# Gate projection of a decoder layer as 2x2x2 blocks with Strassen's seven products

## The chip, the cores and the metric

One core of one Trainium2 chip. The metric is the time on the device, in microseconds, of one execution of the whole program. All data are fp32.

## The reference, cut to what matters

The program is one decoder layer for 512 prompt tokens and 8 sample tokens (520 columns in all, `TOK`). Only the part around the change:

```python
xn = rmsnorm(x, lw['norm1'])
proj = xn @ lw['w_in']            # 1024 features in; q, k, v, ssm and memory columns, then 3072 gate columns
...
gates = sigmoid(proj[..., GATE_COL:]).reshape(bsz, seq, 3, D_MODEL)
merged = gates[:, :, 0] * (att @ w_att_out) + gates[:, :, 1] * (ssm @ w_ssm_out) + gates[:, :, 2] * (mem @ w_mem_out)
h = x + merged @ lw['w_o']
...                               # then a router and 32 experts (w1, w3, w2: 201 MB of weights)
```

## The kernel before, in words

Every engine has one instruction list, written out by hand; semaphores order them, and each engine takes its list strictly in order. SBUF is one tile, `arena`, with places given in KB; PSUM is one tile, `bank`, of 8 banks. Tokens lie on the free axis (520 columns, two halves of `HALF` = 260), features on the partitions.

1. **Projection** (PE line 679): 26 column tiles of 128 by `x_tiles`, then the memory keys and values (line 771), and the S5 branch with its gated unit (lines 782 to 845), with side work on ACT, DVE and POOL.
2. **Gate stage with attention.** The 24 gate tiles (3072 columns) are worked off by `gate_tile` (lines 849 to 858): 8 feature blocks of the weights times two token halves, 16 products of 128x128 by 128x260, which accumulate in banks 0 and 1. ACT copies the tile out in `gate_out` (line 1406) to `gates`. 16 of them stand between the steps of the prompt's attention, two to each of 8 head pairs (lines 901 to 907: `gate_tile`, `turn_probs`, `gate_tile`, `scores` of the next pair, `values`); the other 8 stand between the steps of memory attention, one to each of 8 pairs (lines 921 to 941). The softmax of each pair runs beside a gate tile: on DVE lines 1756 to 1775 (two heads: add the distances, maximum, and after ACT's Exp of line 1413 the scaling of line 1775), in memory attention lines 1796 to 1807. SP loads each gate tile's weights (512 KB) into one of two `ring` buffers (line 439). POOL copies the caches of sample tokens 4 to 7 from DRAM to DRAM beside the first 16 gate tiles (`shift_caches`, line 537, whose waits count `tile`). ACT loads the caches for decode (`load_keys`, lines 398 and 399) after each of the first five memory pairs, and `w_ssm` (2 MB, line 1446) after the sixth.
3. **Decode attention.** ACT applies the sigmoid to all gates in one instruction (line 1450). PE goes through the cached keys of 8 sample tokens (lines 971 to 976), then the values (lines 1004 to 1014), with the S5 output products `ssm_out` (line 952) between them; DVE multiplies those by the gates (`ssm_merge`, line 1814), which frees the banks (`Sfree`). SP loads the later keys, values and output weights (lines 442 to 463).
4. **Output products and merge** (line 1032, DVE lines 1814, 1867, 1868), then `w_o` (line 1041), the norm and router, and the **experts** (lines 1165 to 1203), whose weights SP streams into ten buffers (`HOMES`); the first of them is loaded once the last `ssm_out` is done (line 465), the next once `merged` is complete (line 470).

A row of an fp32 matmul in the trace is half of one: each product of 128x128 by 128x260 has two rows, so that a gate tile has 32.

Of the kernel before, what the change touches and what calls it, by code (L numbers as in the profile page):

```python
# [32 lines left out]
P = 128  # L33
D = 1024
# [43 lines left out]
N_FIRST = N_PROJ + N_MEMT  # L78

# [47 lines left out]
def build(nc, t):  # L127

    with ExitStack() as ctx:
# [98 lines left out]
        kv_dec = at(S5 + 90, NG, 2, ATT)  # L228
        dist0 = at(PROJ, NCLS, SEQ)
        work = S5 + 82  # L230
# [8 lines left out]
        slot = [(PROJ + 16 + 7 * i, PROJ + 19 + 7 * i) for i in range(4)] + [(MK, MK + 12)]  # L239
# [11 lines left out]
        dpv = at(work, NG, 64 * NB)  # L251
# [3 lines left out]
        w_att, w_ssm, w_mem = at(RING, 2, D), at(PROJ, 4, D), at(XN, 4, D)  # L255
# [81 lines left out]
        late = dict(pick=("Sfree", KT), turned=("Sj", KT), placed=("merged", KT), sums=("Pj", 2 * KT),  # L337
# [48 lines left out]
        E_KVD = E_KV + NG  # L386
# [16 lines left out]
        def _(sp):  # L403
# [30 lines left out]

            with sp.Fori(1, (N_FIRST + N_GATE) // 2) as i2:
                for u in range(2):

                    sp.wait_ge(s["tile"], i2 * 2 + (u + 1))
                    sp.dma_start(ring[u], t["w_stream"][bass.ds(i2 * 2 + u, 1)].rearrange(
                        "o p k c -> (o p) k c")).then_inc(s[f"win{u}"], 16)  # L440

            for b in range(NSLOT, NB):
# [17 lines left out]
            sp.wait_ge(s["dvdone"], MH * (NB - 1))  # L460
            sp.dma_start(w_o[1], t["w_o"][:, 4:8, :]).then_inc(s["wo"], 16)
            sp.wait_ge(s["dvdone"], MH * NB)
            sp.dma_start(w_o[0], t["w_o"][:, 0:4, :]).then_inc(s["wo"], 16)
            sp.dma_start(gain_f, t["norm_f"].partition_broadcast(P)).then_inc(s["gainf"], 16)
            sp.wait_ge(s["Sj"], KT)
# [58 lines left out]
        def _(pool):  # L524
            def shift_caches(b0, b1, first):


                with pool.Fori(0, b1 - b0) as i:
                    for part, (groups, kv) in enumerate((((2,), "k"), ((0, 1), "k"), ((2,), "v"), ((0, 1), "v"))):
                        pool.wait_ge(s["tile"], i * 4 + (2 + first + part))  # L530
# [45 lines left out]
            pool.dma_start(dist0, t["dist0"]).then_inc(s["dist0"], 16)  # L576
# [16 lines left out]
            for g in range(NG):  # L593
                for kv, name in ((0, "k"), (1, "v")):
                    pool.dma_start(t[f"sample_swa{g}_{name}"][:, WINDOWS[g] - 1, :], kv_dec[0:NB, g, kv, :]
# [3 lines left out]

            shift_caches(4, NB, N_FIRST + 1)  # L600

# [62 lines left out]
        def _(pe):  # L664
# [162 lines left out]
            for g in range(NG):  # L827
                b = jobs.take_pe(pe)
                for q in range(4):
                    last = pe.transpose(b[0:NB, q * P:(q + 1) * P], proj[:, T_QKV + 6 * g + 2 + q, SEQ:TOK], ident)  # L830
# [68 lines left out]
            pe.wait_ge(s["vrows"], 10)  # L899
            scores(0)  # L900
            for pair in range(NPAIR):
                gate_tile(2 * pair)
                turn_probs(pair)
                gate_tile(2 * pair + 1)
# [16 lines left out]
            for pair in range(NCLS * MH // 2):  # L921
                its = (2 * pair, 2 * pair + 1)
                gate_tile(NCLS * NH + pair)
# [10 lines left out]
                for it in its:  # L934
                    h = it % MH
                    pe.wait_ge(s["mptc"], it + 1)
                    wait_from(pe, s["moc"], it - 1)
                    for q in range(2):
                        last = pe.matmul(bank[:, 6 + it % 2, 0:P], mv_rows[:, q, h * MD:(h + 1) * MD],
                                         pmT[it % 2][:, q * P:(q + 1) * P], start=q == 0, stop=q == 1)  # L940
                    last.then_inc(s["mO"], 1)

            def ssm_out(j):


                if j == 0:
                    pe.wait_ge(s["wssm"], 16)
                    pe.wait_ge(s["ssm"], 4)
                wait_from(pe, s["Sfree"], (0, 1, 2, 0, 0, 4, 5, 6)[j])
                for k in range(4):  # L950
                    for h in range(2):
                        last = pe.matmul(bank[:, SSM_BANK[j] + h, 0:HALF], w_ssm[:, k, j * P:(j + 1) * P],  # L952
# [6 lines left out]
            pe.wait_ge(s["moc"], NCLS * MH)  # L959
            pe.wait_ge(s["gevac"], N_GATE)  # L960
# [32 lines left out]
            pe.wait_ge(s["dbackc"], 3)  # L993
            for g in range(NG):
                for hh in range(2):
                    pe.matmul(bank[32 * hh:32 * hh + 32, 6, 0:P], dpn[0:NB, g, 32 * hh:32 * hh + 32],
                              kv_dec[0:NB, g, 1, hh * P:(hh + 1) * P], start=g == 0, stop=False,
# [1231 lines left out]
```

## Time and profile before

| | |
|---|---|
| time, median of 3 runs | 1201.76 us (1199.83, 1201.8, 1201.76) |
| span of the profiled execution | 1199.0 us (the profile gives its span alone; the three runs lie 0.8 to 2.8 us above it) |
| gate stage beside attention, 289.4 to 436 us | PE busy throughout |
| gate stage beside memory attention, 436 to 512 us | PE busy 75.0 of 76.0 us |
| decode, merge and output products, to 691 us | PE mostly busy |
| experts, 691 to 1160 us | the DMA engines busy throughout from 782 us |

The profile is one execution, its times in us from the first instruction. An engine's line number is that of the kernel's text. The chain of waits is followed back from the last instruction to what released each step, so its rows are what the end hung on; where PE stands in it without a break, PE sets the pace there.

### The profile page before, as it was taken

What the parts mean: (1) busy time and instruction counts of PE and PEld (TensorE: products, weight loads), DVE (VectorE), ACT (ScalarE), POOL (GpSimd) and SP (SyncE); (2) the same over time, 40 slices, a digit from 0 to 9 for tenths busy, and PEclk for the clock granted to TensorE, in tenths of its full rate; (3) what the DMA queues carried; (4) which work ended last, traced back from release to release, by engine and by line L of the source; (5) the groups of instructions that cost most, each with busy time, mean ns of one, the idle gap of its engine ahead of it and who ended that gap; (6) DMA issues with size and microseconds to landing.
All of it is one profiled execution on the core that took longest, in us unless ns stands there. A gap on an engine that the chain in (4) does not pass through costs nothing.

```text
span 1199.0 us, 16688 instructions
## 1 busy us (share of the span) xinstructions
PE 1086.0 (91%) x6915; PEld 778.2 (65%) x6915; DVE 353.6 (29%) x761; ACT 232.3 (19%) x444; POOL 134.8 (11%) x152
## 2 busy tenths in 40 slices
PE   7999999999999999999999879997777788888875
PEld 6888888897888888878855545554444444444441
DVE  3994306923223242231544421010000000000003
ACT  4103021135222222250021211111111111110114
POOL 2113310002000100000000010111111111111010
PEclk9999999999999999999999979999899989999899
DMA  6771367324755654377347389999999999999984
GB/s 226 252 256 54 102 222 237 122 93 153 243 194 197 219 186 170 137 246 302 160 182 277 138 346 403 416 417 419 417 420 419 422 423 421 421 420 420 419 322 147
DMA packets 48938, 330.89 MB, mean 276 GB/s; under 512 B 8860, under 2 KB 12012, under 8 KB 35424
## 3 DMA queue, kind: packets, MB, share of 16 engines
q1 hardware_dynamic: 31744, 257.65, 54.0%
q0 software_dynamic: 15104, 64.44, 15.7%
q10 hardware_dynamic: 2016, 7.76, 1.6%
q8 instruction: 53, 0.87, 0.3%
q14 instruction: 21, 0.17, 0.0%
HBM read 319.77 MB, written 62.11 MB: 318 GB/s over the span
## 4 chain that ended last, share of the span: by engine, by line
PE 66%; DMA 29%; ACT 2%; issue 1%; SPq 1%; DVE 1%; POOLq 0%; ACTq 0%; DVEq 0%
DMA arena<-in_w 25%; PE bank L856 14%; PE bank L679 14%; PE bank L1178 8%; PE bank L1041 5%; PE bank L1203 4%; PE bank L1032 4%; PE bank L952 2%; PE bank L692 1%; PE bank L771 1%; PE bank L845 1%; DMA arena<-in_w_stream 1%; PE bank L871 1%; PE bank L892 1%; ACT arena L1450 1%
## 5 line engine op out<-in xcount | busy, mean ns | idle before, releaser
L1178 PE MATMUL bank<-arena 128*64 128x256 f32 x2048 | 262.4, 413 | 65.5 <-DMA arena<-in_w 64.9
L1178 PEld LDWEIGHTS bank<-arena 128*64 128x64 f32 x2048 | 160.3, 144 | 159.7 <-issue 58.5
L856 PE MATMUL bank<-arena 128*128 128x260 f32 x768 | 173.1, 384 | 0.0
L679 PE MATMUL bank<-arena 128*128 128x260 f32 x768 | 169.9, 383 | 0.0
L679 PEld LDWEIGHTS bank<-arena 128*128 128x128 f32 x768 | 145.4, 190 | 23.0 <-issue 0.5
L856 PEld LDWEIGHTS bank<-arena 128*128 128x128 f32 x768 | 144.1, 190 | 22.4 <-issue 1.2
L1203 PE MATMUL bank<-arena 128*64 128x512 f32 x512 | 115.6, 593 | 3.5 <-DVE arena L2039 3.5
L2033 DVE TENSOR_TENSOR arena<-arena,bank 128x256 f32<-128x256 f32 x32 | 13.5, 422 | 326.5 <-ACT arena L1507 326.5
L635 POOL DMA_INDIRECT y_dram<-arena,scatter_rows x31 | 44.3, 1430 | 384.1 <-ACT arena L1523 350.0
L1203 PEld LDWEIGHTS bank<-arena 128*64 128x64 f32 x512 | 36.7, 136 | 63.4 <-issue 54.4
L1507 ACT ACTIVATE arena<-bank 128x256 f32<-128x256 f32 x32 | 12.3, 384 | 320.5 <-PE bank L1178 320.5
L1523 ACT ACTIVATE arena<-bank,arena 64x512 f32<-64x512 f32 x62 | 42.3, 683 | 103.8 <-PE bank L1203 103.4
L1041 PE MATMUL bank<-arena 128*128 128x512 f32 x128 | 58.7, 601 | 0.0
L1308 ACT ACTIVATE arena<-bank 128x520 f32 (+1 forms) x24 | 14.5, 604 | 150.0 <-PE bank L679 150.0
L1032 PE MATMUL bank<-arena 128*128 128x260 f32 x192 | 42.2, 382 | 0.0
L1032 PEld LDWEIGHTS bank<-arena 128*128 128x128 f32 x192 | 36.5, 190 | 5.6
L2025 DVE TENSOR_TENSOR arena<-bank,arena 128x512 f32<-128x512 f32 x32 | 20.6, 687 | 61.9 <-PE bank L1165 61.9
L1041 PEld LDWEIGHTS bank<-arena 128*128 128x128 f32 x128 | 23.1, 190 | 23.6 <-issue 23.4
L1406 ACT ACTIVATE arena<-bank 128x520 f32<-128x520 f32 x24 | 14.5, 604 | 111.7 <-PE bank L856 111.7
L1763 DVE SCALAR_TENSOR_TENSOR arena<-arena,bank 128x512 f32<-128x512 f32 x16 | 10.9, 683 | 85.4 <-PE bank L871 85.4
L1814 DVE TENSOR_TENSOR arena<-arena,bank 128x520 f32<-128x520 f32 x24 | 16.6, 693 | 54.5 <-PE bank L952 26.2
L1636 DVE TENSOR_TENSOR arena<-arena 128x16 f32<-128x16 f32 (+6 forms) x24 | 13.0, 584 | 60.3 <-ACT arena L1348 59.8
(341 smaller groups left out, 1083.2 us busy)
## 6 DMA issues: line engine op xcount, KB each, us to landing
arena<-in_w SPq DMA_DIRECT2D x95, 2048.0 KB, 35.9
arena<-in_w_stream SPq DMA_DIRECT2D x56, 512.0 KB, 3.5
out_sample_swa_k<-in_cache_swa_k POOLq DMA_DIRECT2D x8, 2047.0 KB, 10.5
out_sample_swa_v<-in_cache_swa_v POOLq DMA_DIRECT2D x8, 2047.0 KB, 10.2
arena<-in_cache_mem_v SPq DMA_DIRECT2D x8, 512.0 KB, 6.4
arena<-in_w_o SPq DMA_DIRECT2D x2, 2048.0 KB, 15.4
out_sample_swa_k<-in_cache_swa_k POOLq DMA_DIRECT2D x8, 511.0 KB, 6.7
out_sample_swa_v<-in_cache_swa_v POOLq DMA_DIRECT2D x8, 511.0 KB, 6.2
```

Source lines behind the costliest of these rows:

```text
L635: pool.indirect_dma_start(out=h_acc, out_offset=bass.IndirectOffsetOnAxis(ap=rows, axis=0), in_=y_sb[e % NYS], in_offset=None, bounds_chec ...
L679: last = pe.matmul(bank[:, 2 * u + h, 0:HALF], ring[u][:, k, :], x[:, k, h * HALF:(h + 1) * HALF], start=k == 0, stop=k == KT - 1)
L856: last = pe.matmul(bank[:, h, 0:HALF], ring[n % 2][:, k, :], xn[:, k, h * HALF:(h + 1) * HALF], start=k == 0, stop=k == KT - 1)
L952: last = pe.matmul(bank[:, SSM_BANK[j] + h, 0:HALF], w_ssm[:, k, j * P:(j + 1) * P], ssmT[:, k, h * HALF:(h + 1) * HALF], start=k == 0, st ...
L1032: last = pe.matmul(bank[:, 2 + 2 * i + h, 0:HALF], w[:, k, j * P:(j + 1) * P], src[:, k, h * HALF:(h + 1) * HALF], start=k == 0, stop=k == ...
L1041: last = pe.matmul(bank[:, 2 * (i % 2) + half, :], gates[:, k, T * P:T * P + P], w_o[k // 4][:, k % 4, half * 512:(half + 1) * 512], start ...
L1178: last = pe.matmul(bank[64 * q:64 * q + CAP, 2 + u, part * FE // 2:(part + 1) * FE // 2], xgT[e // 2 % 2][:, k, 64 * u:64 * u + CAP], w[:, ...
L1203: last = pe.matmul(bank[64 * q:64 * q + CAP, 6 + u, :], hT[u][:, j, par_ * CAP:(par_ + 1) * CAP], down_w[i][:, j, par_, q * 512:(q + 1) * ...
L1308: act.activation(dst, bank[:, 2 * u:2 * u + 2, 0:HALF], ACT.Copy).then_inc(s["evac"], 1)
L1523: last = act.activation(y_sb[v][:, q * 512:(q + 1) * 512], bank[half, 6 + u, :], ACT.Copy, scale=slot_gate[half, e:e + 1])
L1814: return TT(g, g, bank[:, b0:b0 + 2, 0:HALF], ALU.mult)
L2025: TT(xgT[pair % 2][:, 4 * half:4 * half + 4, :], bank[:, half, :].rearrange("p (k a) -> p k a", k=4), wide(gain2_x[:, 4 * half:4 * half + ...
```

## The change

Two gate tiles make a pair (12 pairs). A pair's weights are four quarters, `b11`, `b21`, `b12`, `b22`, each 4 feature blocks by 128 columns (256 KB), and the activations `xn` are four quarters as well (4 feature blocks by 260 tokens). The pair is computed by seven products instead of eight, in the form with fifteen additions (Winograd's):

- **PE**: `gate_step` takes the place of `gate_tile`. The first step of a pair makes products M1, M6, M5, M7, the second M2, M3, M4; each is 4 matmuls of 128x128 by 128x260. M1 and M2 accumulate in bank 0, M6, M7 and M4 in bank 1, M5 and M3 in bank 7. Waits stand before M1, M6, M7, M2, M3 and M4.
- **DVE**: four sums of the activations once (`sum1` to `sum4`, 1040 columns each) behind the copies of the memory values; per pair four combinations of weights (`t1` to `t4`, 512 columns each) and five additions into `gates` (260 columns, one operand in PSUM). `gate_v` stands between the two heads' scalings, the rest behind the second.
- **ACT**: two copies of 260 columns per pair (`first_product`, `gate_out`) in place of two of 520.
- **SP**: four loads of 256 KB per pair in place of two of 512 KB, into eight places that rotate; each waits for a product and for combinations of the pair before. `w_ssm` is loaded by SP in four pieces, after the last product, instead of by ACT. `w_o`'s second half waits for all of `dvdone`, its first half for the last `ssm_out`.
- Attention buffers move: `dist0` keeps 7 blocks of 128 instead of 4x512 (its rows overlap), `kv_dec` has keys and values on different partitions (12 small products in two banks instead of three), `dpv` is three tiles, the cache slots lie elsewhere, and memory attention's output uses bank 6 alone, copied two heads at a time.
- **POOL**: `shift_caches` counts products instead of tiles (1st, 5th, 8th and 12th of each two pairs).

The core of the diff:

```diff
-            def gate_tile(i):
-
-                wait_from(pe, s["gevac"], i)
-                n = N_FIRST + i
-                pe.wait_ge(s[f"win{n % 2}"], 16 * (n // 2 + 1))
-                for k in range(KT):
-                    for h in range(2):
-                        last = pe.matmul(bank[:, h, 0:HALF], ring[n % 2][:, k, :],
-                                         xn[:, k, h * HALF:(h + 1) * HALF], start=k == 0, stop=k == KT - 1)
-                last.then_inc(s["tile"], 1)
+            def product(i, m):
+
+                opens = m in (M1, M6, M5)
...
+                for k in range(4):
+                    last = pe.matmul(bank[:, product_bank[m], 0:HALF], wq[i][left[m]][:, k, :], right[m][:, k, :],
+                                     start=opens and k == 0, stop=k == 3, skip_group_check=True)
+                last.then_inc(later_sem("product"), 1)
+
+            def gate_step(n):
+
+                i, second = divmod(n, 2)
+                parts = 5 * i
+                if not second:
+                    pe.wait_ge(*later("b11", 16 * (i + 1)))
+                    wait_from(pe, s["gevac"], 2 * i)
+                    product(i, M1)
+                    pe.wait_ge(*later("term", TERMS * i + 3))
+                    wait_from(pe, *later("gpart", parts))
+                    product(i, M6)
+                    product(i, M5)
+                    pe.wait_ge(*later("gpart", parts + 1))
+                    product(i, M7)
+                else:
+                    pe.wait_ge(*later("b21", 16 * (i + 1)))
+                    pe.wait_ge(s["gevac"], 2 * i + 1)
+                    product(i, M2)
+                    pe.wait_ge(*later("b22", 16 * (i + 1)))
+                    pe.wait_ge(*later("gpart", parts + 3))
+                    product(i, M3)
+                    pe.wait_ge(*later("term", TERMS * (i + 1)))
+                    product(i, M4)
...
+            for i in range(1, N_PAIR):
+                done = PRODUCTS * (i - 1)
...
+                sp.wait_ge(*later("product", done + M1 + 1))
+                sp.wait_ge(*later("term", TERMS * (i - 1) + 3))
+                load_quarter(i, "b11")
+                load_quarter(i, "b12")
+                sp.wait_ge(*later("product", done + M6 + 1))
+                sp.wait_ge(*later("term", TERMS * i))
+                load_quarter(i, "b22")
+                sp.wait_ge(*later("product", done + M2 + 1))
+                load_quarter(i, "b21")
+            sp.wait_ge(*later("product", PRODUCTS * N_PAIR))
+            for k in range(4):
+                sp.dma_start(w_ssm[k], t["w_ssm"][:, k, :]).then_inc(s["wssm"], 16)
...
+            def terms(i):
+
+                w = wq[i]
+                for name in ("b12", "b22", "b11"):
+                    dve.wait_ge(*later(name, 16 * (i + 1)))
+                if i:
+                    dve.wait_ge(*later("product", PRODUCTS * (i - 1) + M7 + 1))
+                TT(w["t3"], w["b22"], w["b12"], ALU.subtract).then_inc(later_sem("term"), 1)
+                dve.wait_ge(*later("term", TERMS * i + 1))
+                TT(w["t1"], w["b12"], w["b11"], ALU.subtract).then_inc(later_sem("term"), 1)
+                dve.wait_ge(*later("term", TERMS * i + 2))
+                TT(w["t2"], w["b22"], w["t1"], ALU.subtract).then_inc(later_sem("term"), 1)
+
+            def last_term(i):
+                w = wq[i]
+                dve.wait_ge(*later("b21", 16 * (i + 1)))
+                if i:
+                    dve.wait_ge(*later("product", PRODUCTS * (i - 1) + M3 + 1))
+                dve.wait_ge(*later("term", TERMS * i + 3))
+                TT(w["t4"], w["b21"], w["t2"], ALU.subtract).then_inc(later_sem("term"), 1)
+
+            def gate_v(i):
+                dve.wait_ge(s["gevac"], 2 * i + 1)
+                dve.wait_ge(*later("product", PRODUCTS * i + M6 + 1))
+                TT(v_tmp, s1_tmp, bank[:, product_bank[M6], 0:HALF], ALU.add).then_inc(later_sem("gpart"), 1)
...
                     TS(prob[odd], prob[odd], rd, None, ALU.mult).then_inc(s["pn"], 1)
+                    if odd == 0:
+                        gate_v(pair)
+                last_term(pair)
+                gate_c22(pair)
+                terms(pair + 1)
+                gate_c12(pair)
+                gate_c21(pair)
```

In memory attention (`it` counts heads, four to a gate pair) DVE takes `gate_v`, `last_term`, `gate_c22` behind the second head and `terms` of the next pair, `gate_c12`, `gate_c21` behind the fourth. `gate_c22` waits for M7 and makes two additions, `gate_c12` waits for M3, `gate_c21` for M4.

## Rows read from the trace of the kernel before

**Rows 1.** Busy time by stretch: us; busy (x count) per engine; PE clock; DMA share; GB/s.
```profile
184.00:289.40 105.40, 101.86 (x750) 88.35 (x748) 62.15 (x80) 29.74 (x62) 12.67 (x23) 1.00 0.48 160
289.40:436.00 146.60, 146.60 (x874) 123.10 (x876) 47.22 (x104) 39.80 (x80) 12.79 (x22) 1.00 0.58 199
436.00:512.00 76.00, 74.96 (x404) 65.72 (x405) 23.68 (x87) 19.14 (x58) 1.11 (x2) 1.00 0.41 148
782.00:1160.00 378.00, 310.02 (x2084) 171.00 (x2082) 35.09 (x73) 43.58 (x75) 47.17 (x36) 0.94 1.01 418
```

**Rows 2.** Chain of waits: first tile, one attention pair, one memory tile: start us, us, what.
```profile
290.96 7.21 PE bank L856 x32
...
327.96 7.21 PE bank L856 x32
...
336.48 7.01 PE bank L856 x32
...
346.46 7.21 PE bank L856 x32
...
448.28 7.02 PE bank L856 x32
```

**Rows 3.** Chain of waits, behind the gate stage.
```profile
503.53 7.03 PE bank L856 x32
511.76 1.28 ACT L1450
513.05 10.61 ACT arena L1450
523.75 0.71 DVE arena L1814
524.50 3.77 PE bank L952 x16
...
564.96 42.08 PE bank L1032 x192
```

**Rows 4.** DVE in order of time, the softmax of one attention pair.
```profile
326.60 0.69 DVE L1763 SCALAR_TENSOR_TENSOR arena<-arena,bank 128x512 f32<-128x512 f32 x1 [12.29 <-PE bank L871]
331.19 0.62 DVE L1775 TENSOR_SCALAR arena<-arena 128x768 f32<-128x768 f32 x1
332.18 0.62 DVE L1775 TENSOR_SCALAR arena<-arena 128x768 f32<-128x768 f32 x1
```

**Rows 5.** DVE additions: one operand in PSUM (page), both in SBUF (order of time).
```profile
L2033 DVE TENSOR_TENSOR arena<-arena,bank 128x256 f32<-128x256 f32 x32 | 13.5, 422 | 326.5 <-ACT arena L1507 326.5
...
571.05 0.70 DVE L1867 TENSOR_TENSOR arena<-arena 128x520 f32<-128x520 f32 x1
```

**Rows 6.** Gate weight loads by their line, 289 to 512 us, 512 KB each.
```profile
DMA to landing us min/median/max: 3.4/3.6/6.3
```

**Rows 7.** DMA issues, 289 to 436 us: the largest cache copy (KB, us to landing).
```profile
out_sample_swa_k<-in_cache_swa_k POOLq DMA_DIRECT2D x4, 2047.0 KB, 10.5
```

**Rows 8.** DVE in order of time: ahead of the gate stage, and its first pair.
```profile
278.84 0.70 DVE L1745 TENSOR_TENSOR arena<-arena 128x520 f32<-128x520 f32 x1 [7.72 <-ACT arena L1400]
...
295.93 0.62 DVE L1775 TENSOR_SCALAR arena<-arena 128x768 f32<-128x768 f32 x1
```

**Rows 9.** DVE in order of time: the turn from attention to memory attention.
```profile
438.09 1.34 DVE L1780 MEMSET arena<- 128x1536 f32 x1 [0.27 <-issue]
444.79 0.35 DVE L1807 TENSOR_SCALAR arena<-arena 128x256 f32<-128x256 f32 x1
```

**Rows 10.** Chain of waits: PE at that turn.
```profile
439.07 7.01 PE bank L856 x32
```

**Rows 11.** The one load of w_ssm by its tensor, 2048 KB.
```profile
DMA to landing us min/median/max: 9.5/9.5/9.5
```

**Rows 12.** PE in order of time: first ssm_out, last keys before the second.
```profile
517.72 3.77 PE L952 MATMUL bank<-arena 128*128 128x260 f32 x16
523.19 0.60 PE L974 MATMUL bank<-arena 128*32 128x256 f32 x6
```

More of the change, by code:

```diff
@@ L78 @@
 N_FIRST = N_PROJ + N_MEMT
+QUARTER = D // 2
+N_PAIR = N_GATE // 2
+PRODUCTS = 7
+TERMS = 4
+FIRST_HALF = 4
+M1, M6, M5, M7, M2, M3, M4 = range(PRODUCTS)
+START_OF_STEP = (0, FIRST_HALF, PRODUCTS, PRODUCTS + FIRST_HALF)
 KB = 256
@@ L227, in build, with quarters @@
         k_rows = [at(S5 + x, NCLS, ATT) for x in (82, 86, 18)]
-        kv_dec = at(S5 + 90, NG, 2, ATT)
-        dist0 = at(PROJ, NCLS, SEQ)
-        work = S5 + 82
+        kv_dec = at(S5 + 93, NG, ATT)
+        dist0 = at(PROJ, 7 * P)
+        work = S5 + 81.75
+        xq = {"11": xn[:, 0:4, 0:HALF], "12": xn[:, 4:8, 0:HALF], "21": xn[:, 0:4, HALF:TOK],
+              "22": xn[:, 4:8, HALF:TOK]}
+        vals = [at(PROJ + (T_QKV + 6 * g + 4) * TOK / KB, 4, HALF) for g in range(NG)]
+        sum1, sum2, sum4, sum3 = vals[0], vals[1], vals[2], xq["21"]
+        homes_q = [at(kb, 4, P) for kb in (RING, RING + 2, RING + 4, RING + 6, PROJ + 4, PROJ + 6, S5 + 91, MK + 6)]
+        s1_tmp, v_tmp, w_tmp = (at(S5 + 87.75 + 1.015625 * i, HALF) for i in range(3))
+        def quarters():
+            names = ("b11", "b21", "b12", "b22", "t2", "t3", "t4", "spare")
+            now = dict(zip(names, homes_q))
+            places = []
+            for _ in range(N_PAIR):
+                places.append(dict(now, t1=now["b12"]))
+                now = dict(b11=now["spare"], b12=now["b11"], b22=now["t2"], t3=now["b12"], t2=now["t3"],
+                           b21=now["b21"], t4=now["b22"], spare=now["t4"])
+            return places
+        wq = quarters()
+        right = [{M1: xq["11"], M6: sum2, M5: sum1, M7: sum3, M2: xq["12"], M3: sum4, M4: xq["22"]}[i]
+                 for i in range(PRODUCTS)]
+        left = [{M1: "b11", M6: "t2", M5: "t1", M7: "t3", M2: "b21", M3: "b22", M4: "t4"}[i]
+                for i in range(PRODUCTS)]
+        product_bank = [{M1: 0, M2: 0, M6: 1, M7: 1, M4: 1, M5: 7, M3: 7}[i] for i in range(PRODUCTS)]
         prob = [at(work + 3 * i, 6 * P) for i in range(2)]
@@ L234, in build @@
         pmT = [at(MK + 4, MEM), at(MK + 5, MEM)]
-        slot = [(PROJ + 16 + 7 * i, PROJ + 19 + 7 * i) for i in range(4)] + [(MK, MK + 12)]
+        slot = [(PROJ + 8.25, PROJ + 11.25), (PROJ + 20.5, PROJ + 23.5), (PROJ + 32.75, PROJ + 35.75),
+                (PROJ, work + 2), (MK, MK + 12)]
         slot_k = [at(x, NG, 2, P) for x, _ in slot]
@@ L250, in build @@
         dpn = at(MK + 17, NG, 64)
-        dpv = at(work, NG, 64 * NB)
+        dpv = [at(x, 64 * NB) for x in (work, S5 + 91, MK + 6)]
         dmpv = at(PROJ + 45, 2, MH, 32 * NB)
         do_rows, dmo_rows = at(S5 + 59, P), at(work + 6, P)
-        w_att, w_ssm, w_mem = at(RING, 2, D), at(PROJ, 4, D), at(XN, 4, D)
+        w_att, w_mem = at(RING, 2, D), at(XN, 4, D)
+        w_ssm = [at(PROJ + (T_QKV + 6 * g + 4) * TOK / KB, D) for g in range(NG)] + [at(PROJ + 4, D)]
         w_o = [at(HOMES[6], 4, D), at(HOMES[8], 4, D)]
@@ L335, in h_back_in @@
                 (kdec[T], 32 * len(range(T, NB, NSLOT)) + 16)
-        late = dict(pick=("Sfree", KT), turned=("Sj", KT), placed=("merged", KT), sums=("Pj", 2 * KT),
+        late = dict(product=("cplx", 2), term=("toep", CH), gpart=("sprev", 3), xsum=("uscaled", 1),
+                    b11=("x0", 16), b12=("x1", 16), b21=("x2", 16), b22=("x3", 16), pick=("Sfree", KT), turned=("Sj", KT), placed=("merged", KT), sums=("Pj", 2 * KT),
                     added=("Pfree", 2 * KT))
@@ L1743, in _, with gate_c21 @@
+            def gate_c21(i):
+                dve.wait_ge(*later("product", PRODUCTS * i + M4 + 1))
+                TT(gates[:, 2 * i, HALF:TOK], s1_tmp, bank[:, product_bank[M4], 0:HALF], ALU.add
+                   ).then_inc(later_sem("gpart"), 1)
+            dve.wait_ge(s["yadd"], 4)
+            terms(0)
             for ct in range(4):
@@ L1807, in _ @@
                 TS(pm[b], pm[b], rd, None, ALU.mult).then_inc(s["mpn"], 1)
-            for it in range(NCLS * MH - 2, NCLS * MH):
-                mo_copy(it)
+                i = NPAIR + it // 4
+                if it % 4 == 1:
+                    gate_v(i)
+                    last_term(i)
+                    gate_c22(i)
+                if it % 4 == 3:
+                    if i + 1 < N_PAIR:
+                        terms(i + 1)
+                    gate_c12(i)
+                    gate_c21(i)
+            mo_copy(NCLS * MH // 2 - 1)
             def times_gate(tile, b0):
@@ L1819, in ssm_merge @@
                 times_gate(3 * j + 1, SSM_BANK[j]).then_inc(s["Sfree"], 1)
-            then(dve.memset(dpv, 0.0), dve.memset(dmpv, 0.0))
+            then(*[dve.memset(x, 0.0) for x in dpv], dve.memset(dmpv, 0.0))
             dve.wait_ge(s["gsig"], 1)
```

151 lines of the change are left out of this document (103 added, 48 removed).

## Prediction

> **What bounds the kernel now.** I read the chain of waits first, for who sets the pace where the change is made. From 289.4 to 512 us it consists of PE alone: two gate tiles of 7.21 and 7.01 us to an attention pair, whose period is 346.46 - 327.96 = 18.50 us, and one of 7.02 us to a memory pair [rows 2]. There are 8 pairs of either kind, so 24 tiles. The busy time by stretch says the same: PE works 146.6 of 146.6 and 75.0 of 76.0 us, at the full granted clock (1.00, the 2.4 GHz level), while DVE has 47.2 and 23.7 us of work in them [rows 1]. So the stage gets shorter by whatever matmul time leaves it, if DVE and the loads keep up.
>
> Behind it the chain goes over ACT's sigmoid (1.28 us table, 10.61 us), DVE's first multiplication, PE [rows 3], and from 782 us over the loads of expert weights, with DMA fully busy [rows 1]. Those loads start when PE passes `ssm_out(7)` and the merge, not at a fixed time: a DMA-bound end that starts earlier ends earlier. Nothing else is pending there, since the cache copies run beside the first 16 tiles only. A gain in the gate stage should reach the end whole.
>
> **Parts, one by one.**
>
> *Matmuls.* A tile's 32 rows take 7.01 us, 0.219 each; the 7.21 of the tile behind `values` holds 0.2 more at its start, which stays [rows 2]. A pair has 7 products of 8 rows, 1.754 us each, 12.28 us where it was 14.03. Gain: 1.754 x 12 = **21.05 us**. Does a wait between products cost something by itself? The output products have such waits every 8 or 16 rows, and their 192 rows take 42.08 us, again 0.219 each [rows 3]: a wait that is already met costs nothing.
>
> *DVE in attention.* New per pair: four weight terms of 512 columns, 0.70 us by the 520-column row, and five additions of 260, 0.42 us by the 256-column one [rows 5], so 4.9 us per pair, 59 us over the stage. The sum fits into DVE's idle time (it waits 12.29 us per pair for scores [rows 4]), but the order matters. M7 waits for `gate_v`, which stands behind the first head's scaling. That ends 3.85 us after the pair's gate work begins (331.81 - 327.96 [rows 2, 4]); `gate_v` is done by 4.3. M1, M6, M5 take 0.2 + 3 x 1.754 = 5.46 us, so the wait is met with 1.1 us to spare. Nothing on PE waits; zero.
>
> *The ring through SP.* In DVE's list, `terms` of the next pair stands ahead of `gate_c12`, `gate_c21` and the next softmax, and waits for quarter `b22`, which SP may only load once `last_term` is done. From the start of a softmax: second scaling done at 6.2 (332.80 - 326.60 [rows 4]), `gate_v` 0.45, `last_term` 0.7, so 7.35; then the landing L, three terms at about 0.73 and two additions at 0.43, 3.1 together: the ring takes 10.5 + L. PE's new period is 18.50 - 1.75 = 16.75, so the ring is hidden as long as L is below 6.2 us. No row shows a load of 256 KB. The nearest, 512 KB on the same queue beside the same cache copies, took 3.4 to 6.3 us, median 3.6 [rows 6]; half the bytes should stay below the median, and I take 3.5: zero. The far end is a cache copy's own 10.5 us [rows 7].
>
> *Memory attention.* Same products and terms, in the slots behind second and fourth heads. Between `last_term` and the next `terms` lie M5, M7, M2 and M3, 7.0 us, and memory attention's own steps, so that even the slowest load of [rows 6] is there in time: zero, except at the turn below.
>
> *First pair.* The first softmax has no `values` ahead of it: the scaling ends at 296.55 [rows 8], M5 ends at 290.96 + 5.4 = 296.3 [rows 2]. ACT's new copy stands between its two exponentials, off that path; `gate_v` ends near 297.0. M7 waits: **+0.75**.
>
> *Turn to memory attention.* DVE clears the decode buffers and then takes both heads, until 444.79 + 0.35 = 445.14 [rows 9]; `gate_v` comes behind that, 445.6. PE starts at 439.07 [rows 10] and is through M5 at 444.35. M7 waits: **+1.35**.
>
> *Ahead of the stage.* Four sums of 1040 columns (about 1.25 us each, twice the 520-column row of 0.70 less its fixed part, an estimate from [rows 5]) and three terms, 7.1 us, are covered by the gated unit's matmuls, during which DVE idles 7.72 us ahead of its first product and more between them [rows 8]. They end near 280.5; the last product stays where it was. Zero; without that cover 7 us. The merged `kv_dec` jobs are the same 12 small matmuls and four ACT copies for three, there too: zero, bounds -0.5 and +0.5.
>
> *SP, POOL, ACT.* SP issues four loads per pair and has nothing else to do; the POOL copies keep their pace; ACT copies the same columns or fewer. Quarters `b11`, `b12`, `b21` are issued over half a pair ahead. Zero. The sigmoid now waits for `gate_c21`, 0.65 us behind M4; before, ACT was busy 1.2 us behind the last tile anyway (510.56 to 511.76 [rows 3]): zero.
>
> *`w_ssm`.* It used to land in attention's shade; now SP asks for it when the last product ends (E, which was 510.56). The first `ssm_out` came at E + 7.2 [rows 12]. The only row for 2 MB took 9.5 us [rows 11], but beside a gate tile's 0.5 MB. Of the 6.1 us by which it is longer than the shortest small load [rows 6], a fifth is that tile's by its bytes; so I take 9.5 - 1.2 = 8.3 (an estimate), plus 0.1 for the issue. So `ssm_out(0)` starts 1.3 late. It need only be ready when the sigmoid and the first multiplication are: two keys' work lies between, ending at 523.79, and the second `ssm_out` started at 524.50 [rows 12, 3]. Of 1.3 us, 0.7 vanish: **+0.55**. Ends: 0 (landing under 7.8) and +1.8 (9.5). The Trainium skill, page "DMA: Bandwidth & Descriptors", section on the anatomy of one DMA, fits a transfer as 2.0 us plus its bytes over 436 GB/s; by that (an estimate) 2 MB land in 6.8 us, `ssm_out` waits for nothing and the sum is 0.55 us better. The fit is for the other kind of queue, and the row here was slower, so the sum stays with the row. SP's keys for samples 5 to 7 queue behind `w_ssm`, 5 us of transfers; those are due from E + 13 on, the values from E + 32: zero.
>
> *`w_o`, `dpv`, `dist0`.* `w_o`'s halves are issued some 2 and 8 us later but wanted 45 us behind that, and they precede the same loads in the same queue: zero. Three copies into `dpv` for one cost 0.3 us beside `ssm_out(4)`: zero.
>
> **Sum.** -21.05 + 0.75 + 1.35 + 0.55 = -18.4 us against a profiled span of 1199.0, so 1180.6. The median of the runs stands 2.8 above that span: 1201.76 - 18.4 = **1183.4 us**, 1.5% faster.
>
> **Rivals.**
> 1. *The ring is only half hidden.* If the quarter waits for the running cache copy, L becomes about 7.5 (the copy's 10.5 [rows 7], less the 4 us by which M1, which starts it, is ahead of `last_term`, plus a us of its own): 8 x (7.5 - 6.2) = 10 us back, **1194**. For it: copies and loads share the DMA engines and are triggered by the same products. Against: 512 KB never took over 6.3 [rows 6]. Chance 0.13.
> 2. *The ring becomes the bound: slower.* The same place, DVE's wait for `b22` in `terms`. It decides against the kernel once 8 x (L - 6.2) exceeds 18.4 + 2.4, so from L = 8.8. With the 9.5 of `w_ssm` [rows 11] for a quarter, 8 x 3.3 = 26 us, **1210**. Against: a quarter is an eighth of those bytes. Chance 0.06.
> 3. *The waits open gaps.* If each of the 84 products began like the tile behind `values`, 0.2 us late [rows 2], 17 us go back: **1200**. Against: the output products' 0.219 [rows 3]. Chance 0.05.
> 4. *The clock falls.* In the stretch from 184 us PE idles 3.5 us and the clock shows 1.00; with the experts it idles 68 of 378 us and shows 0.94 [rows 1]. Waits of 2.1 us in all should leave it at the upper level. At 1.2 GHz for a third of the products the stage would lose 147 / 3 = 49 us, **1232**. The Trainium skill, page "TensorE: Matmul & The Clock Gate", section on psum-queue depth-cycling, states that cycling through PSUM banks made the engine idle briefly between groups so often that the clock oscillated; seven groups in three banks resemble that, and the rows here show no such fall. Chance 0.01.
>
> That the products don't get fewer I exclude: seven of four matmuls stand in the text for eight.
>
> **Numbers.** The forecast has 0.75. The range goes from 1179.5 (no stall at all, 1180.7, less a us of scatter) to 1195, which takes in rival 1; what is left out is rivals 2 to 4 and a tail. Faster by over 0.2% (2.4 us, about what a measurement here can tell from no change): 0.75 + 0.13 + a little of 3, 0.89. Within: 0.04 from rival 3. Slower: 0.07.
>
> **What would show it.** 672 matmul rows for the gate products in place of 768, still 0.219 us each; attention period near 16.75 us; PE waiting once near 297 and once near 445 us for DVE, nowhere else over 0.3 us; `terms` waiting on DVE for `b22` but the next softmax still starting by its scores; loads of 256 KB at 3 to 4 us; `ssm_out(0)` waiting about a us for `w_ssm`; expert loads all some 18 us earlier. I am wrong if the period stays above 17.5, if DVE's softmax starts behind its scores, or if the expert loads don't move with the gate stage.

## The result, and the profile after

The changed kernel takes 1192.76 us (median of 4 runs, 1189.68 to 1193.56) beside 1201.01 for the kernel before (4 runs): 0.9927 of it, 95% interval 0.9911 to 0.9943. It is 8.3 us faster; the forecast was 18.4, with 1183.4 us.

The profiled execution took 1192.96 us, its span 1191.3 (before: 1199.0). Split at the same marks, the spans compare as follows (in us; the changes are taken before rounding). The marks are the starts of the first `scores`, the first memory scores and the first attention output product, and the end of the gate stage's last product.

| stretch | before | after | change | forecast |
|---|---|---|---|---|
| up to `scores(0)` | 289.4 | 291.3 | +1.9 | 0 |
| attention | 148.6 | 141.4 | -7.2 | -13.3 |
| memory attention | 72.6 | 67.0 | -5.6 | -5.7 |
| last product to first output product | 54.2 | 56.3 | +2.0 | +0.55 |
| rest | 634.2 | 635.3 | +1.1 | 0 |

The first and the last line are scatter. The nine experiments below on the changed kernel, which leave the work up to there alone, had `scores(0)` between 288.6 and 290.9 us, and the rest varied between 630.7 and 635.5 us in them. What calls for an explanation is attention, where 6.1 us of the forecast gain are missing, and the 1.5 us behind the gate stage.

Busy time by stretch of the changed kernel: attention, memory attention, and the way to the output products. The columns are those of [rows 1].

```profile
291.30:432.00 140.70, 135.33 (x832) 111.65 (x832) 82.12 (x176) 36.14 (x81) 13.95 (x24) 1.00 0.68 217
432.00:499.80 67.80, 66.09 (x346) 57.82 (x343) 38.80 (x114) 15.88 (x54) 0.00 (x0) 1.00 0.35 116
499.80:556.00 56.20, 51.64 (x557) 42.05 (x556) 12.97 (x33) 15.75 (x12) 0.00 (x0) 1.00 0.82 299
```

Where PE worked all of 146.6 us [rows 1], it now idles 5.4 of 140.7. DVE, which should have been the suspect, is busy for 82 of them. The clock stayed at its upper level (1.00). The groups of instructions, PE between 291 and 500 us, first row, and DVE in attention (busy us, mean ns, then the idle time just ahead of them and what ended it):

```profile
L929 PE MATMUL bank<-arena 128*128 128x260 f32 x672 | 153.8, 385 | 6.6 <-DVE arena L1883 6.6
...
L1866 DVE TENSOR_TENSOR arena<-arena 128x512 f32<-128x512 f32 x8 | 5.5, 692 | 45.7 <-DMA arena<-in_w_stream 45.7
```

All 672 rows of the gate products are there (84 products of 8 rows), and whatever PE lost ahead of one it lost to `gate_v` (L1883), the addition that M7 waits for. DVE lost 45.7 us in 8 waits, one to a pair, ahead of the first weight term (L1866), and there it waited for a quarter of the stream. The chain of waits in one pair joins the two, here from the issue of `b22` (start, us, what):

```profile
334.38 9.39 DMA arena<-in_w_stream
...
343.85 0.70 DVE arena L1866
...
346.66 0.60 DVE arena L1924
...
351.70 0.43 DVE arena L1883
...
352.18 2.02 PE bank L929 x8
```

`b22` takes 9.39 us to land. The terms (L1866) stand behind it, the next softmax (L1924) behind them, `gate_v` (L1883) behind that, and M7 starts only when it is done. PE in order of time shows the price, with the wait in brackets:

```profile
352.18 2.02 PE L929 MATMUL bank<-arena 128*128 128x260 f32 x8 [1.63 <-DVE arena L1883]
```

The product that had to wait also takes 2.02 us from its first start to its last end, where products in a stream follow each other every 1.754. About 0.1 us of the difference is its first row, which takes 0.49 us instead of 0.38, its weights being loaded only when the wait is over; the rest is the end of a row, which in a stream overlaps with the next. M7 waits like this in the first pair, as forecast, and in four others.

The loads of the stream and the largest cache copies in attention (count, KB each, median us to landing; then the loads' shortest, median and longest):

```profile
out_sample_swa_k<-in_cache_swa_k POOLq DMA_DIRECT2D x4, 2047.0 KB, 11.4
out_sample_swa_v<-in_cache_swa_v POOLq DMA_DIRECT2D x4, 2047.0 KB, 10.7
```
```profile
DMA to landing us min/median/max: 2.6/3.5/9.7
```

The median of 3.5 us is what the prediction took for every quarter. But the 32 loads are four different ones. `b11` and `b12`, issued just ahead of the copy, land in 2.8 to 3.9 us. `b22`, issued 2.8 to 5.9 us behind its start, took 7.9, 6.6, 9.4, 5.1, 9.7, 6.2, 8.9 and 5.8, mean 7.46, and in each of the eight pairs it landed 0.2 to 1.8 us behind the copy. That is the prediction's first rival, with its L of about 7.5.

That it stands in a queue can be seen in the packets. In the pair shown `b22` is issued at 334.38, and the packets that the DMA engines moved from 334.4 to 338.5 us are all of the copy's queue (packets, MB, share of 16 engines):

```profile
q0 software_dynamic: 163, 1.33, 102.7%
```

The first packet of `b22` starts 4.1 us behind its issue; in the eight pairs that is 1.8 to 4.5 us, without the copies (experiment 1) 0.95.

The landings alternate, and so do the periods from the second pair on: 17.8 to 18.8 us, then 16.75. A landing of 7.9 to 9.7 us makes DVE late, so the next `b22` is issued later in its pair (10.6 to 11.6 us behind its scores instead of 8.7 to 9.2), further into the copy, and lands in 5.1 to 6.6.

### The profile page after: what moved, and what is told of

Same layout as the page of the kernel before. It is cut to its first block, busy times and chain, and to the rows that moved or that the text cites. A ratio compares the mean times of both kernels' runs of the same rounds, so it can differ in the third digit from the quotient of the medians.

```text
span 1191.3 us, 16670 instructions
## 1 busy us (share of the span) xinstructions
PE 1067.3 (90%) x6831; PEld 760.5 (64%) x6831; DVE 410.9 (34%) x869; ACT 226.6 (19%) x445; POOL 135.4 (11%) x153
## 4 chain that ended last, share of the span: by engine, by line
PE 54%; DMA 36%; DVE 5%; issue 2%; ACT 1%; SPq 1%; POOLq 0%; ACTq 0%; DVEq 0%
DMA arena<-in_w 25%; PE bank L749 14%; PE bank L1278 8%; DMA arena<-in_w_stream 7%; PE bank L929 5%; PE bank L1141 5%; PE bank L1303 4%; PE bank L1132 4%; PE bank L1051 2%; PE bank L762 1%; PE bank L841 1%; DVE arena L1929 1%; PE bank L920 1%; DVE arena L1924 1%; DMA hn_dram<-arena 1%
## 5 line engine op out<-in xcount | busy, mean ns | idle before, releaser
L1278 PEld LDWEIGHTS bank<-arena 128*64 128x64 f32 x2048 | 160.2, 143 | 159.6 <-issue 54.1
L749 PE MATMUL bank<-arena 128*128 128x260 f32 x768 | 170.1, 383 | 1.6 <-DMA arena<-in_w_stream 1.6
L749 PEld LDWEIGHTS bank<-arena 128*128 128x128 f32 x768 | 145.4, 190 | 24.7 <-DMA arena<-in_w_stream 2.0
L929 PE MATMUL bank<-arena 128*128 128x260 f32 x672 | 153.8, 385 | 6.6 <-DVE arena L1883 6.6
L929 PEld LDWEIGHTS bank<-arena 128*128 128x128 f32 x672 | 125.3, 190 | 28.5 <-DVE arena L1883 9.0
L1303 PEld LDWEIGHTS bank<-arena 128*64 128x64 f32 x512 | 37.0, 136 | 63.5 <-issue 54.2
L1132 PE MATMUL bank<-arena 128*128 128x260 f32 x192 | 42.2, 382 | 0.0
L1132 PEld LDWEIGHTS bank<-arena 128*128 128x128 f32 x192 | 36.5, 190 | 5.6
L1141 PEld LDWEIGHTS bank<-arena 128*128 128x128 f32 x128 | 23.1, 190 | 23.6 <-issue 23.4
L1051 PE MATMUL bank<-arena 128*128 128x260 f32 x128 | 29.7, 387 | 2.2 <-DMA arena<-in_w_ssm 2.2
L841 PE MATMUL bank<-arena 128*128 128x256 f32 x128 | 28.9, 383 | 1.0 <-DMA arena<-in_w_stream 1.0
```

Of the source, the lines that this page charges most:

```text
L749: last = pe.matmul(bank[:, 2 * u + h, 0:HALF], ring[u][:, k, :], x[:, k, h * HALF:(h + 1) * HALF], start=k == 0, stop=k == KT - 1)
L841: last = pe.matmul(bank[:, 2 * u, 0:MEM], ring[u][:, k, :], memn[:, k, :], start=k == 0, stop=k == KT - 1)
L929: last = pe.matmul(bank[:, product_bank[m], 0:HALF], wq[i][left[m]][:, k, :], right[m][:, k, :], start=opens and k == 0, stop=k == 3, skip ...
L1051: last = pe.matmul(bank[:, SSM_BANK[j] + h, 0:HALF], w_ssm[k][:, j * P:(j + 1) * P], ssmT[:, k, h * HALF:(h + 1) * HALF], start=k == 0, st ...
L1132: last = pe.matmul(bank[:, 2 + 2 * i + h, 0:HALF], w[:, k, j * P:(j + 1) * P], src[:, k, h * HALF:(h + 1) * HALF], start=k == 0, stop=k == ...
L1141: last = pe.matmul(bank[:, 2 * (i % 2) + half, :], gates[:, k, T * P:T * P + P], w_o[k // 4][:, k % 4, half * 512:(half + 1) * 512], start ...
```

## Experiments

The theory (A): `b22` queues behind the running 2 MB copy, so the ring of loads and additions sets the pace of attention. Rivals: (B) DVE's longer list does; (C) PE loses the time itself, around each product.

**1. No copies beside the gates.**
```diff
-            shift_caches(4, NB, 0, True)
...
```


> Left out: the copies of samples 4 to 7 of the decode caches that run beside the gate stage (their rows of the cache outputs are not written). Theory A (the 6 us that attention gave back are the ring: each pair's b22 is issued while a 2 MB cache copy runs and lands only with it, 7.5 us after its issue on average where 6.2 is free): b22 lands 3 to 4.5 us after its issue, DVE's terms stop waiting for the stream's quarters (45.7 us in 8 waits now), the attention stage falls from 141.4 to 135 to 136.5 us and the kernel to 1186 to 1188 us. Rival B (DVE's longer in-order list, the additions and the softmax of a pair, is the bound): the stage stays at 141 us and the time at 1192 to 1193. Rival C (PE loses the time itself, in the waits and weight loads around each block product): also 141 us and 1192 to 1193.

Measured: 1184.73 us, ratio 0.9863 (0.9847 to 0.9880). Attention took 135.35 us; `b22` landed in 2.8 us on average.

**2. The copies half a pair later.** Each pair of cache copies is started by products; `START_OF_STEP` says by which.
```diff
-START_OF_STEP = (0, FIRST_HALF, PRODUCTS, PRODUCTS + FIRST_HALF)
+START_OF_STEP = (FIRST_HALF, PRODUCTS, PRODUCTS + FIRST_HALF, 2 * PRODUCTS)
```


> Nothing is left out; the same copies in the same order, each set off half a pair later, so that the 2 MB copy starts at M2 instead of M1 and b22 (issued after M6) meets the small copy or none, while b21 (issued after M2) meets the large one. Theory A: b22 lands 3 to 5 us after its issue; b21, which is wanted only by M2 of the next pair, takes 6 to 10 without harm; the stage falls to 135.5 to 138 us, the time to 1186.5 to 1189.5. Rivals B and C: the stage stays at 141 us, the time at 1192 to 1193. If b21's delay is what the ring then waits for, M2 to M4 wait instead and the time stays too, but then the trace has the wait at the terms of the second half.

Measured: 1181.59 us, ratio 0.9850 (0.9822 to 0.9878). Attention 135.34 us, `b22` 4.0 us on average. Nothing is left out, and the edit is four numbers. Of the 11 us by which the time lies under the changed kernel's, attention holds 6.1; the rest lies outside it, where the edit changes nothing, and is scatter.

**3. A ninth home, `b22` issued with `b11` and `b12`.**
```diff
...
-                sp.wait_ge(*later("product", done + M6 + 1))
-                sp.wait_ge(*later("term", TERMS * i))
+                if i > NPAIR:
+                    sp.wait_ge(*later("product", done + M6 + 1))
+                    sp.wait_ge(*later("term", TERMS * i))
                 load_quarter(i, "b22")
+                if i <= NPAIR:
+                    sp.wait_ge(*later("term", TERMS * i))
```


> A ninth home for a quarter (free memory ahead of the vectors of attention) lets b22 be issued together with b11 and b12, ahead of the large copy, for the eight turns of attention; the copies stay where they are. Theory A: b22 lands 4 to 5.5 us after its issue and 8 us earlier than now, DVE's terms no longer wait for it, the stage falls to 135 to 137 us and the time to 1186 to 1188.5. If the copy delays whatever is under way beside it and not only what is issued behind it, b11 and b12 slow too and the gain is half. Rivals B and C: 141 us, 1192 to 1193.

Measured: 1183.99 us, ratio 0.9856 (0.9840 to 0.9873), attention 135.34 us. The landing was not as expected: issued some 0.1 us behind the copy in seven of eight pairs, `b22` still took 8.5 us on average. It does not matter, since it was asked for 3 to 4.5 us earlier in the pair. So it is not the time to landing that costs, but where it falls in the ring.

The three stages are as theory A has them. The three times lie 1.3 to 4.9 us under the ranges expected by it, by such scatter.

Busy time by stretch for attention of these three, in their order (columns as above):

```profile
288.80:424.11 135.31, 134.28 (x832) 112.09 (x833) 84.76 (x177) 36.82 (x81) 0.00 (x0) 1.00 0.20 63
```
```profile
288.60:423.95 135.35, 134.32 (x832) 112.12 (x833) 84.61 (x177) 36.81 (x81) 13.04 (x22) 1.00 0.67 213
```
```profile
290.10:425.44 135.34, 134.31 (x832) 112.07 (x833) 83.70 (x177) 36.70 (x81) 13.90 (x24) 1.00 0.69 224
```

Three different edits end at 135.3 us. DVE does the same 84 us of work in each, and PE has the same products with the same waits on their semaphores: B and C fall. The second and third move the same bytes at about the same rate as the changed kernel (213 and 224 GB/s for 217), so it is not bandwidth either, but order.

**4. `w_ssm` earlier.**
```diff
-            sp.wait_ge(*later("product", PRODUCTS * N_PAIR))
-            for k in range(4):
+            for k in (0, 1, 3, 2):
+                if k in (0, 2):
+                    sp.wait_ge(*later("product", PRODUCTS * (N_PAIR - 1) + (M5 if k == 0 else M3) + 1))
                 sp.dma_start(w_ssm[k], t["w_ssm"][:, k, :]).then_inc(s["wssm"], 16)
```


> The four pieces of w_ssm are loaded as the last pair's quarters leave their homes (three after M5, the last after M3) and not after its last product. Theory: the first ssm_out then starts 7.2 us after the gate stage's end as in the kernel before (9.46 now) and the time falls by 1.6 to 2.2 us, to 1190.6 to 1191.2. Rival: the wait for w_ssm only uncovers the next one (the chain of DVE's combine and ACT's sigmoid and table load, 7.03 after the end before), and the gain is under 0.5 us; or the early pieces delay the last pair's own loads, which would show as a wait of its products.

Measured: 1186.32 us, ratio 0.9875 (0.9859 to 0.9892), 6.4 us better where 2 were expected. The first `ssm_out` came 7.03 us behind the last product (9.29 in the changed kernel), the output products at 54.1 (56.3): 2.2 us, as expected. The rest came from elsewhere: attention took 138.3 us with nothing changed in it. So I ran the changed kernel again.

**5. The changed kernel again.**

> The changed kernel itself, unaltered, beside the next three on one chip. The run that loaded w_ssm earlier gained 6.4 us where 2 were expected; its trace has 2.2 us of that behind the gate stage, 3.1 in attention (138.3 us for 141.4, with nothing changed there) and 0.9 ahead of it. Theory A (the ring's loads queue behind the running copy, and by how much depends on when copy and load happen to meet): the stage of this kernel is not fixed; a second profile shows 137.5 to 142 us, with b22's mean time to landing moving with it (6.2 to 7.5 us), and the time 1188 to 1193. If instead the stage comes out at 141.4 within 0.3, then the 3.1 us belong to the earlier w_ssm in a way not understood.

Measured: 1189.93 us (6 runs, 1186.80 to 1194.04), ratio 0.9904 (0.9881 to 0.9926), attention 140.8 us, `b22` 7.33 us on average. Neither 141.4 to the tenth nor as low as 138.3: the stage's length goes with the landings, in the order of their means (7.16, 7.33 and 7.46 us for 138.3, 140.8 and 141.4). That the 138.3 of experiment 4 is chance as well is not shown by this, since two executions of one kernel differ by 0.6 us here; shown is that its loads landed earlier. Attention without the collision repeats within 0.01 us (135.34 and 135.35 us).

**6. Copies later and `w_ssm` earlier together** (the edits of 2 and 4).

> The copies half a pair later and w_ssm earlier, together; nothing left out. If the two are independent: the attention stage at 135.3 us, the first ssm_out 7.0 us after the stage's end, the time 2.0 to 2.4 us under that of the copies alone (1181.6): 1179 to 1180, and 9 to 13 us under the changed kernel on the same chip. Rival: the end of the kernel scatters by more than that (1178.9 to 1185.8 in four runs of one kernel) and the gain does not show in the time, only in the stages.

Measured: 1183.82 us, ratio 0.9846 (0.9825 to 0.9868). The stages are as expected (attention 135.35 us, the first `ssm_out` 7.03 us behind the last product). The time is not under that of 2: the rival was right that it scatters more than the 2 us in question. It is told by the stages only.

**7. And the turn.** In addition to the edits of 6, DVE's preparation of the decode operands goes into the memory heads.
```diff
-            dve.wait_ge(s["dprod"], 1)
-            then(dve.memset(dq, 0.0), dve.memset(dmq, 0.0), dve.memset(newprod, 0.0))
...
                     last_term(i)
+                    if it > 4:
+                        clear(it // 4 - 1)
                     gate_c22(i)
```


> As the last one, and VectorE's preparation of the decode operands (the memsets, copies and products that stand between attention's last additions and memory's first) is spread over the memory heads, so that the turn to memory attention no longer waits for it. Theory: the 1.2 us for which TensorE waits there for gate_v go to 0 and nothing else moves: 1.0 to 1.4 us under the previous run. Rival: a memory head is shorter on VectorE than on TensorE by less than the work put into it, and the waits come back in the memory stage (67.0 us now), or the first decode product waits.

Measured: 1181.72 us, ratio 0.9838 (0.9819 to 0.9857). The memory stage fell from 67.03 to 65.56 us, so by 1.47. The first rows are PE in order of time at the turn in the changed kernel, the second the chain of waits at the same place here:

```profile
435.63 3.45 PE L929 MATMUL bank<-arena 128*128 128x260 f32 x15
440.28 2.02 PE L929 MATMUL bank<-arena 128*128 128x260 f32 x8 [1.19 <-DVE arena L1883]
```
```profile
425.08 1.10 PE bank L1012 x4
426.18 7.01 PE bank L930 x32
```

The product M7, which waited 1.19 us and then took 2.02, is now one of four in a row. Of all versions tried, this one has the lowest ratio to the kernel before, and nothing is left out; by its time it can't be told from 2 and 6.

**8. The copies two products later.**
```diff
-START_OF_STEP = (0, FIRST_HALF, PRODUCTS, PRODUCTS + FIRST_HALF)
+START_OF_STEP = (2, FIRST_HALF + 2, PRODUCTS + 2, PRODUCTS + FIRST_HALF + 2)
```


> The changed kernel with every copy set off two block products (3.5 us) later instead of four. b22 is issued 8.7 us after a pair's scores in the undisturbed schedule, the large copy then at 9.3. Theory A (what counts is that the load is issued ahead of the copy, not how far): b22 lands 2.6 to 4.5 us after its issue, b21, issued 4 us behind the copy's start, takes 6 to 8 without harm, the stage is 135.3 to 136.5 us and the time that of the half pair's shift. If the copy slows any load that is under way beside it: b22 takes 5 to 7, the stage lies between 136.5 and 140.

Measured: 1199.40 us (12 runs), ratio 0.9981 (0.9968 to 0.9993): 9.5 us slower than the changed kernel on the same chip, all but back at the kernel before. Attention took 151.2 us. The chain of waits:

```profile
298.46 9.38 DMA arena<-in_w_stream
...
307.92 0.70 DVE arena L1866
...
310.73 0.60 DVE arena L1924
...
317.59 9.15 DMA arena<-in_w_stream
```

and POOL's issue of the copy in the second of these pairs:

```profile
315.37 0.63 POOL L605 DMA_DIRECT2D out_sample_swa_v<-in_cache_swa_v  x1 [7.64 <-PE bank L929]
```

I had the mark wrong. In the first pair of the changed kernel the copy starts 4.4 us behind `scores(0)`, not 5.7 to 5.9 as in all later ones, where `values` stands between the scores and M1. 3.5 us more put it at 8.0, and `b22` is issued at 9.0. So it met the copy near its beginning, the worst place of those tried. In a later pair, undisturbed, `b22` would have been issued at 8.7 and the copy at about 9.3, an estimate from the same marks. But it stayed behind the copy. From one issue of `b22` to the next the ring takes its landing plus 317.59 - 298.46 - 9.38 = 9.75 us. The sum of 19.1 us is longer than PE's 16.75, so PE waits, the next copy is triggered late, and the next `b22` meets it again, 0.7 to 2.2 us into it in every pair. Here the landings are 7.4 to 10.1 us, mean 8.83, within -0.2 to +0.5 us of the copy's own.

**9. The copies three products later** (3 in the place of 2).

> Every copy set off three block products later than in the changed kernel (two made it 9 us slower, four 11 us faster). What the three traces have in common under theory A: a b22 issued behind the large copy's start lands when the copy does, so its time to landing is what is left of the copy's 10 us; the late b22 delays the terms, whose end is what the next b22 waits for, so the ring keeps its lag. In an undisturbed pair b22 is issued 8.7 to 9.1 us after the pair's scores. Two products put the copy at 8.0 to 8.8, just ahead of it; three put it at 9.8 to 11, just behind. So by theory A one product more takes all of it back: b22 lands in 2.5 to 4 us, b21, issued 3 us behind the copy's start, takes 6 to 8 without harm, the stage falls from 151.2 to 135.3 to 135.8 us, the time is 1180 to 1185. Rival: any load beside the copy's first half is slowed, whichever is ahead, and a copy in the middle of a pair is bad in itself: the stage stays above 140 and the time above 1188.

Measured: 1183.95 us, ratio 0.9870 (0.9851 to 0.9890), attention 135.34 us, as expected. One product, 1.75 us, took back 15.9. Busy time in attention of experiment 8, then of this one:

```profile
289.40:440.66 151.26, 137.28 (x833) 111.15 (x833) 82.37 (x177) 36.02 (x81) 14.02 (x24) 1.00 0.66 200
```
```profile
288.80:424.10 135.30, 134.27 (x833) 112.08 (x833) 84.71 (x177) 36.81 (x81) 12.97 (x22) 1.00 0.69 217
```

In the view of POOL's issues POOL now starts the copy at 332.68, where SP had issued `b22` at 330.24:

```profile
332.68 0.62 POOL L605 DMA_DIRECT2D out_sample_swa_k<-in_cache_swa_k  x1 [4.12 <-PE bank L929]
```
```profile
330.24 0.33 SPq L483 DMA_DIRECT2D arena<-in_w_stream  x1
```

The landings of that `b22` and of the `b21` issued at 334.91, behind the copy's start, by the line of the loads:

```profile
DMA to landing us min/median/max: 3.8/3.8/3.8
...
DMA to landing us min/median/max: 8.0/8.0/8.0
```

The delay has only changed its victim. `b21` is due a pair later, and nobody waits for it.

**10. The kernel before, without the copies.**
```diff
-            shift_caches(4, NB, N_FIRST + 1)
...
```


> The kernel before without the cache copies of samples 4 to 7 beside its gate stage (their rows of the cache outputs are not written). It tells whether the copies cost the kernel before anything, and so what the change is worth where no copy runs. If the kernel before hid its loads behind its own slack (two whole tiles ahead; its second load of a pair lands in 4.1 to 6.3 us beside the copy): attention stays at 148.4 to 148.6 us and the time at 1199 to 1201.5; the change without copies is then worth 15 to 16.5 us. Rival: the copies slow attention in the kernel before too, by some 2 us and more, and the change's own worth is smaller.

Measured: 1201.04 us, ratio 1.0007 (0.9995 to 1.0019), attention 148.59 us as with them:

```profile
289.80:436.40 146.60, 146.60 (x874) 123.11 (x876) 47.20 (x104) 39.80 (x80) 0.00 (x0) 1.00 0.17 55
```

Where they stand in the kernel before, the copies cost it nothing. The loss belongs to the change alone, which gave them something to be in the way of.

## Why the prediction was wrong, and where it was right

**The step that failed** is the ring through SP, in the sentence "half the bytes should stay below the median, and I take 3.5: zero". The row behind it, 3.4 to 6.3 us for 512 KB [rows 6], is in attention two populations. Of the two loads of a pair one was issued 0.6 to 0.8 us ahead of the copy and landed in 3.4 to 3.5 us; the other came some 7.5 us behind the copy's start and took 4.1 to 6.3. A `b22` comes 2.8 to 5.9 us behind it, took 7.46 us on average where 3.5 was put in, and cost 6.1 us where nothing was. I scaled the row by bytes when what decides is the moment of issue. Without copies the quarter takes 2.8 us (experiment 1). The Trainium skill, page "DMA: Bandwidth & Descriptors", section on the anatomy of one DMA, fits 2.0 us plus bytes over 436 GB/s, for loads issued by GpSimd; for 256 KB that is an estimate of 2.6, and the trace agrees, for a load issued by SP. Behind the copy it takes what the copy has left. The Trainium skill, the same page, section on queues, rings and completion order, says that each engine takes turns between its queues and drains a whole packet, typically 9 to 17 descriptors, before it switches. How many such packets the copy makes no run here shows, so the rule leaves open how long a quarter waits behind it; in experiment 8 it lands with the copy, within half a microsecond.

**Rival 1** had the mechanism, and its L (7.5; measured 7.46), at a chance of 0.13. Its price of 10 us was too high, because the ring's own part was: 10.5 us where the chain shows 9.75. So a landing is free up to 16.75 - 9.75 = 7.0 us, not 6.2. Four of the eight landings of the changed kernel exceed 7.0, by 7.9 us together. PE lost 6.1 against the forecast; the difference is not traced.

**Rival 2**, the ring as the bound of a kernel no faster than before, "from L = 8.8", is what experiment 8 made: L of 8.83 and 1199.4 us.

**Behind the gate stage** the term was +0.55 and measured +2.0. The last piece of the load took 7.9 us where 8.3 was forecast for the whole. But I put the issue at 0.1 us, and four pieces are issued one behind the other; the last went out 1.35 us after the last product. The rows are the chain of waits of the changed kernel:

```profile
501.10 7.90 DMA arena<-in_w_ssm
509.04 3.77 PE bank L1051 x16
515.11 3.70 PE bank L1051 x16
```

Of the lateness only the forecast 0.7 us vanished: the second `ssm_out` came 15.3 us behind the last product instead of 13.9 [rows 3]; another 0.7 us was lost further on, where the chain in both kernels waits for the last cached values (`cache_mem_v`). They land 47.4 us behind the last product instead of 45.4. Part of this is scatter: in the seven profiled executions that load `w_ssm` in this way the stretch took 54.3 to 57.2 us, mean 56.3. With the wait away (experiment 4) it is the sigmoid's chain that ends last, and the second `ssm_out` follows it, at 13.7 us:

```profile
497.94 10.62 ACT arena L1559
...
508.63 0.71 DVE arena L1994
...
509.34 0.04 issue
509.38 2.68 PE bank L1052 x11
```

**What held.** *Matmuls*: attention undisturbed is 148.59 - 135.35 = 13.24 us shorter, forecast 14.03 - 0.75 = 13.28; memory attention 5.55, forecast 7.02 - 1.35 = 5.67. So rival 3, gaps at products whose wait is met, is out. *The turn*: 1.35 forecast (the two times given there, 445.6 and 444.35, are 1.25 apart), 1.47 by experiment 7. *The clock* stayed where it was, so rival 4 is out. *The sum*: with the copies out of the way (2 and 9) the kernel takes 1181.6 and 1183.95 us; 1183.4 was forecast. The sum was right, within the scatter of the kernel's end, for a kernel that did not have the collision; the 1.5 us by which the term behind the gate stage was short do not show in it.

**My own marks.** I had said that I would be wrong if the period stayed above 17.5 us, if DVE's softmax started behind its scores, or if the expert loads did not move. The second is what the trace shows: DVE waits for scores ahead of two softmaxes in eight; in experiment 2 ahead of all eight. The first mark was passed narrowly: from the second scores to the last the period is 17.6 us on average, in experiment 2 it is 16.75.

**What stays open:** landings of 5 and of 9 us alternate with how far into the copy `b22` is issued, but why their means differ between executions is not settled. A `before` with its copies moved onto its loads was not tried.

## What to carry to other kernels

A time to landing belongs to a moment of issue, not to a size. Before a row's median is used, split it by what was under way when each load went out, and see which of them somebody waits for. When slack that used to hide loads (here two whole tiles ahead) is traded for a tight ring, write the ring down as its fixed part plus the landing, and find the largest transfer that can stand ahead of it on the same DMA engines. If there is one, let it start behind the load that is due first: here the choice of the product that starts a copy was worth between 0 and 16 us. And try more than one place for such a trigger, since a shift by half of the right amount was worse than none.

## What was not expected of the hardware

A 256 KB load issued 0.7 to 2.2 us behind the start of a 2 MB copy on another queue landed with the copy, 7.4 to 10.1 us after its issue; issued 1.5 to 2.4 us ahead of it, it took 2.9 to 4.4. Issued 0.02 to 0.14 us behind it, it landed 1.4 to 3.9 us ahead of the copy's end (experiment 3). Behind the copy, the first packet of a quarter started 1.8 to 4.8 us after its issue, without a copy 0.95. A wait on PE cost 0.27 us more than its own length: the turn's 1.19 us became 1.47. And a late ring keeps itself late: since the copies go by products and the load by DVE's additions, the collision of the first pair in experiment 8 was followed by one in each of the other seven.
